# Alternating the expert value products between two PSUM banks in a split-precision decoder step

## What is computed

```python
u = u_tab[idx]
act = jax.nn.gelu(jnp.einsum('thkd,td->thk', u, hb).astype(jnp.float32))
v = v_tab[idx].astype(jnp.float32)
return jnp.einsum('thk,thkd->td', gate * act, v).astype(h.dtype)
...
x = x + peer(...)
y_prompt = rmsnorm(xp, g_final)
y_sample = rmsnorm(xs, g_final)
```

## Time and profile before

| what | value |
|---|---|
| median of 3 runs | 3912.73 us (3909.43 to 3913.63) |
| the profiled execution, device time | 3916.97 us |
| its span, first to last instruction | 3915.2 us |
| mean granted TensorE clock | 0.953 |
| TensorE matmuls | 22880, busy 3628.9 us |
| first and last start of L1602 (the value products) | 2750.6 us and 3888.1 us |

### The profile page before, as it was taken

How to read it: one execution, slowest core, us unless ns; L and a number is a source line. 1 busy time by engine, 2 the same in 40 slices (tenths; PEclk the granted TensorE clock), 3 DMA queues, 4 the chain that set the end, 5 groups by cost and what they waited for, 6 DMA issues and landing times. The chain is left out here.

```text
span 3915.2 us, 59057 instructions
## 1 busy us (share of the span) xinstructions
PE 3628.9 (93%) x22880; PEld 3394.9 (87%) x22880; DVE 2037.1 (52%) x3687; ACT 1089.9 (28%) x1197; POOL 2002.8 (51%) x959
## 2 busy tenths in 40 slices
PE   8999868688699799998999999998899999999997
PEld 8988734354699799998999999998899999999997
DVE  4212164121700499677544444444577777777773
ACT  3111122122411322333333333333222222222222
POOL 3333136400433445655566656565576666767662
PEclk9999879777899899999999999999999999999999
DMA  5577767434322223666677777767877877878772
GB/s 212 214 288 290 212 187 212 142 100 136 130 97 97 77 86 110 226 254 238 245 284 288 267 271 288 281 270 273 298 285 295 304 287 285 300 296 297 294 290 104
DMA packets 272840, 891.50 MB, mean 228 GB/s; under 512 B 101105, under 2 KB 134386, under 8 KB 195698
## 3 DMA queue, kind: packets, MB, share of 16 engines
q1 hardware_dynamic: 197458, 548.33, 40.7%
q0 software_dynamic: 36864, 268.45, 16.7%
q10 hardware_dynamic: 38368, 72.83, 5.2%
HBM read 818.45 MB, written 68.71 MB: 227 GB/s over the span
## 5 line engine op out<-in xcount | busy, mean ns | idle before, releaser
L111 POOL TENSOR_TENSOR wl<-raw,wh 128x2048 fp32r<-128x2048 f32 x324 | 1530.0, 4722 | 1373.7 <-ACT wh L107 1373.7
L107 ACT ACTIVATE wh<-raw 128x2048 fp32r<-128x2048 f32 x324 | 620.4, 1915 | 2092.1 <-PE acc L1273 730.4
L1602 PE MATMUL acc<-vh,wh 128*128 128x392 f32 x2048 | 703.5, 343 | 42.2 <-DVE xt L1667 21.2
L1271 PE MATMUL acc<-hh,wh 128*128 128x392 f32 x2048 | 711.5, 347 | 1.8 <-POOL wl L111 1.8
L1272 PE MATMUL acc<-hl,wh 128*128 128x392 f32 x2048 | 700.1, 342 | 0.0
L1273 PE MATMUL acc<-hh,wl 128*128 128x392 f32 x2048 | 697.7, 341 | 0.0
L1603 PE MATMUL acc<-vl,wh 128*128 128x392 f32 x2048 | 696.1, 340 | 0.0
L1604 PE MATMUL acc<-vh,wl 128*128 128x392 f32 x2048 | 695.2, 339 | 0.0
L126 PE MATMUL acc<-hh,wh 128*128 128x264 f32 x1984 | 567.2, 286 | 18.0 <-POOL hl L956 17.2
L127 PE MATMUL acc<-hl,wh 128*128 128x264 f32 x1984 | 561.6, 283 | 0.0
L128 PE MATMUL acc<-hh,wl 128*128 128x264 f32 x1984 | 560.1, 282 | 0.0
(11 more groups left out here) (309 smaller groups left out, 4022.1 us busy)
## 6 DMA issues: line engine op xcount, KB each, us to landing
raw<-units SPq DMA_DIRECT2D x324, 1024.0 KB, 4.8
kr<-cache_k SPq DMA_DIRECT2D x128, 512.0 KB, 6.0
vr<-cache_v SPq DMA_DIRECT2D x256, 256.0 KB, 3.2
expert_acts<-ast ACTq DMA_DIRECT2D x128, 196.0 KB, 2.9
expert_gates<-gs ACTq DMA_DIRECT2D x14, 1792.0 KB, 6.3
a<-expert_acts SPq DMA_DIRECT2D x32, 784.0 KB, 8.9
g<-expert_gates SPq DMA_DIRECT2D x32, 784.0 KB, 11.2
xt<-x_t SPq DMA_DIRECT2D x4, 1040.0 KB, 11.4
```

Of the source, the lines that this page charges most:

```text
L107: act.activation(m.wh[s][:, :, :], m.raw[s][:, :, :], ACT.Copy).then_inc(m.hi_done, 1)
L111: pool.tensor_tensor(m.wl[s][:, :, :], m.raw[s][:, :, :], m.wh[s][:, :, :].bitcast(F32), ALU.subtract).then_inc(m.lo_done, 1)
L1271: pe.matmul(o, m.wh[s][:, k, :], m.hh[:, k, NA:T], start=(k == 0), stop=False)
L1602: pe.matmul(o, m.wh[s][:, 4 * e + d, :], vh[gg][:, e, :], start=(e == 0), stop=False)
```

## The change

The loop over four output tiles becomes a loop over two pairs, `d0` = 0 and 2. Within a pair, each kind of product is done for tile `d0` and then for tile `d0 + 1`, so that two products in a row have the same moving operand, other weights and another PSUM bank. The two waits of a pair become one, for the later of the two counts. `tile_done` is raised by the last product of each tile; these two products now stand next to each other at the end of the pair. The number of matmuls, their sizes, the order of additions within one output tile, and the program of all other engines stay the same.

```diff
-                        for d in range(4):
-                            r = i * 32 + (16 * gg + 4 * n + d)
-                            pe.wait_ge(S["sum_added"], r + 1)
-                            o = m.acc[:, d // 2, d % 2, 0:ND]
+                        for d0 in (0, 2):
+                            pe.wait_ge(S["sum_added"], i * 32 + (16 * gg + 4 * n + d0 + 2))
                             for e in range(GRP):
-                                pe.matmul(o, m.wh[s][:, 4 * e + d, :], vh[gg][:, e, :], start=(e == 0), stop=False)
-                                pe.matmul(o, m.wh[s][:, 4 * e + d, :], vl[gg][:, e, :], start=False, stop=False)
-                                mm = pe.matmul(o, m.wl[s][:, 4 * e + d, :], vh[gg][:, e, :], start=False, stop=(e == GRP - 1))
-                            mm.then_inc(S["tile_done"], 1)
+                                for w, v in ((m.wh[s], vh[gg]), (m.wh[s], vl[gg]), (m.wl[s], vh[gg])):
+                                    last_product = e == GRP - 1 and w is m.wl[s]
+                                    for d in (d0, d0 + 1):
+                                        mm = pe.matmul(m.acc[:, d // 2, d % 2, 0:ND], w[:, 4 * e + d, :], v[:, e, :], start=(e == 0 and w is m.wh[s] and v is vh[gg]), stop=last_product)
+                                        if last_product:
+                                            mm.then_inc(S["tile_done"], 1)
```

## The result

| | before | changed |
|---|---|---|
| median of 20 runs each, us | 3912.71 (3905.09 to 3918.68) | 3919.43 (3913.31 to 3926.64) |
| ratio, 95% interval | | 1.0019 (1.0012 to 1.0025) |
| span of the profiled execution, us | 3915.2 | 3923.4 |
| mean granted clock | 0.953 | 0.953 |

The changed kernel is slower: by 0.19% by the ratio, by 6.7 us by the medians. The value products run from 2751.8 to 3896.6 us, 1144.8 us; before it was 2750.6 to 3888.4 us, 1137.8 us. So 7.0 us of the 8.2 us between the two spans are in this stage, and 1.2 us were there before it began.

A forecast was written before the change was run, and what follows sets the result against it. The value-product stage was taken as bound by TensorE's 0.178 us pace and its waits for VectorE's additions. Pace 0, waits +8.0 and other costs 0 us gave +8.0 us: median about 3921 us, range 3907 to 3932 us.

The forecast's parts named there:

- Pace, value 0 with bounds of 11 us each way: TensorE's value products: changing bank at every product leaves the 0.178 us step unchanged; 0 us, bounds -11 and +11 us.
- Rival A: Value products: writing the same bank costs time, so alternating gains; 3821 us, weak form 3904 to 3910 us; chance 0.13.
- 0.47 us for each blocked group: TensorE's restart behind a VectorE operation held up by GpSimd: it waits for two additions, not one, 0.47 us later.
- the two delays of a group don't add up: Blocked group's two restarts: the second long operation is anchored to GpSimd, so the group loses 0.47 us once.
- 17 groups: Count of groups with VectorE's low part blocked, from its 118.7 us in 31 instances; 17 x 0.47 = 8.0 us.
- rival B: Blocked groups turn free because times shift, soaking up the delay; four of 17 make the sum 0, 3913 us; chance 0.14.
- The other groups don't wait: Free groups: VectorE's weighting still starts ahead of GpSimd, by 0.96 us, despite two additions before it; no cost.
- the second pair is in time: Tiles 2 and 3 are added before TensorE wants them, 1.1 us to spare in a blocked group; wait stays hidden.
- Rival C: Second addition lets GpSimd go first in the 14 free groups, 2.0 us each; 3949 us, or 3935 with half; chance 0.10.
- Rival D: TensorE's clock falls to 1.2 GHz for 24 products at each of 17 waits; 61 us, 3982 us; chance 0.02.

The follow-up runs named there:

- experiment 1: Kernel before, old tile-by-tile product order, but TensorE waits for both banks of a pair before tiles 0 and 2; ratio 1.0018, 7 us.
- experiment 3: Kernel before with second and third product of each block exchanged, so the moving operand repeats within one bank; ratio 0.9994, no difference.
- experiment 2: Changed kernel's alternating order, but each bank has its own wait before its own first product; ratio 1.0014 to the kernel before, 5.5 us.
- experiment 9: Kernel before with gathered rows of units 1 and 2 added behind the weighting and low part, gates loaded as before; ratio 1.0172, 67 us slower.
- experiment 4: Changed kernel with all four tiles of a unit alternating and one wait for all four banks; ratio 1.1791 to the kernel before, 701 us.
- experiment 8: Changed kernel with gates and activations loaded one unit earlier and rows of units 1 and 2 behind weighting and low part; ratio 0.9924, median 3884.76 us.
- experiment 5: Kernel before with the next group's activations and gates loaded one unit earlier; ratio 0.9984, 6 us faster.

## Why the prediction was right

The time was forecast as 3921 us and is 3919.43 us; +8.0 us were forecast and +6.7 us measured. The mechanism, a wait for the second addition in blocked groups, is what experiment 1 shows. That the size came out so well is in part luck: by the trace the waits are 6.0 us and not 8.0 us, and the pace adds 1.5 us where 0 was put, so two misses make up for each other. Step by step:

- **Pace, value 0 with bounds of 11 us each way.** The bounds held, the value was off by little. The undisturbed step averages 178.11 ns instead of 177.87 ns, 1.5 us in the stage, and experiment 3 clears the repeated operand of it. Rival A (3821 us, or 3904 to 3910 us) is out: in four orders of products, with a bank change at every twelfth product or at every one, between two banks or among four, the step is 0.178 us at full clock.
- **0.47 us for each blocked group.** Experiment 1 isolates it: 8.3 us more idle in 17 groups is 0.49 us each. The claim that the two delays of a group don't add up held too, as the second restart keeps its 0.95 us.
- **17 groups.** Here the count was off. (109.0 - 31 x 1.78) / 3.92 = 13.7, and since two of them are blocked in part only, it is 15 in the profiled execution of the changed kernel. The missing two are the bit of rival B that happened, at two places where a free group follows a free one. One of them, VectorE and then GpSimd:

```profile
3056.93 1.79 DVE L1630 TENSOR_TENSOR a<-a,g 128x1568 f32<-128x1568 f32 x1 [1.11 <-DMA g<-expert_gates]
```

```profile
3056.96 6.25 POOL L111 TENSOR_TENSOR wl<-raw,wh 128x2048 fp32r<-128x2048 f32 x1 [2.87 <-ACT wh L107]
```

  The weighting started 0.03 us ahead of GpSimd and went through in 1.79 us, and now GpSimd's subtraction took 6.25 us instead of 4.6 us; the other place has the same 0.03 us. In most blocked groups of the trace of before the weighting started 0.02 to 0.32 us behind. So the count hangs on a race between the gates' landing and GpSimd. Experiment 1, with the same wait, and experiment 2, with the same order of products, both kept 17, so neither alone turned the two; one profile each can't tell it from a change between executions.
- **The other groups don't wait, and the second pair is in time.** Held. The free groups' weighting takes 1.79 us, and restarts in front of a second pair appear only behind a double row, three times 1.1 us where the trace of before has two in front of tile 2.
- **Rival C** (free groups turn blocked) didn't come as a whole: no group is added to the count, though two free ones change places with blocked neighbours. Outside the two places above, the free weightings start 0.79 to 1.28 us ahead of GpSimd, or over 5 us ahead, where 0.96 us was worked out.
- **Rival D** (the clock falls) didn't come in the changed kernel, whose stage is granted 1.00 up to the last group. There a wait of 8.04 us between starts goes with a short stretch at half the clock, in the kernel before as well; the prediction's rows end before it. Experiments 9 and 4 show where it matters: with idle times of 2.55 us in most groups stretches of the stage are at 0.95 to 0.98, with 3.8 us in each unit at 0.85. The Trainium skill, page TensorE: Matmul & The Clock Gate, section on psum-queue depth-cycling, tells of a kernel that cycles through banks and in which TensorE idles between its groups often enough for the clock to swing. The traces agree on the idling: the products that switch banks each time run at full clock as long as no such wait comes, and experiment 9 has the swing with the old order.

The forecast put 0.47 on slower by over 0.2% and 0.39 on within 0.2%. With 0.19% and an interval from 0.12 to 0.25%, the result lies across the line between them.

## What to carry to other kernels

Before two accumulators are interleaved, ask what the interleaving does to the hand-over and not only to the products: both are taken and given back together, so the producer waits for the slower of the two, and the consumer sees both late. Look for the operation behind which the consumer runs late; here it was one that two engines can't do at once, and taking that away was worth over four times what the order of products cost. When an operation is moved, ask what is put in front of whom: the same move gave 0.7% in one setting and took 1.7% in another.

## What the runs showed of the hardware that was not expected

- A VectorE operation with two SBUF inputs is held up for as long as GpSimd's subtraction runs (6.04 us instead of 1.78 us), and when VectorE starts first, by as little as 0.03 us, it is the subtraction that is held up (6.25 us instead of 4.6 us). A row addition with one input from PSUM is not held up: it takes 2.34 to 2.36 us in all these traces, also in the 50 of the kernel before that overlap a subtraction by over 1 us.
- With two banks alternating, the pace depends a little on which buffer holds the moving operand: groups by turns 34.29 and 34.12 us (experiment 8), 178.6 ns a product with `vh0` and `vl0` and 177.7 ns with `vh1` and `vl1`; the changed kernel has 178.6 and 177.6 ns. In the old order both are 34.15 us. So the loss of pace is all in every other group. The cause is open.
- Waits of up to 1.72 us between starts in the middle of the stage leave the granted clock at 1.00 in the changed kernel. Of two waits of 2.25 and 2.51 us in experiment 5, the first was followed by a stretch at half the clock and the second wasn't. In experiment 9, 23 waits of 2.88 us or more brought 17 such stretches, and in experiment 4 the wait in each unit, which then lasts about 14 us, brings the mean down to 0.85: some 200 us of that run's 701 us.
